# Two decoder layers on one core: buffer addresses, the order of transposes, copies and small loads at four places, and the last outputs by column halves

## The reference

```python
for i in range(2):
    h = rms_norm(x, attn_norm[i])
    proj = h @ w_in[i]                       # 1024 x 3072, six units of 512 columns
    sb = rms_norm(stick_breaking(sb_q, sb_k, sb_v), sb_out_norm[i])        # 8 heads of 64
    df = rms_norm(differential(df_q, df_k, df_v, bias, lam), diff_subln[i]) * (1 - lambda_init)
    x = x + concat(sb, df) @ w_out[i]
    h2 = rms_norm(x, ffn_norm[i])
    x = x + (swiglu(h2, dense...) if i == 0 else moe_top2_of_8(h2, router_w, experts...))
return rms_norm(x, final_norm)
```

## Time and profile before

| | |
|---|---|
| time, median of 3 runs | 1462.85 us (1462.66 to 1463.01) |
| the profiled execution's own time | 1462.97 us |
| its span (first to last instruction) | 1460.8 us, so 2.2 us lie around it |
| mean granted TensorE clock | 0.994 of full speed |
| TensorE, VectorE, ScalarE busy | 98%, 77%, 64% of the span |
| DMA | 448.81 MB, 307 GB/s over the span |

### The profile page before, as it was taken

The page is one execution under the profiler, slowest core; times in us unless marked ns, Lnnn a source line. Parts: engine busy times, 40 slices in busy tenths (PEclk is TensorE's granted clock), DMA queues, the critical chain, the costliest instruction groups (busy, mean ns, idle before and its releaser), DMA issues.

```text
span 1460.8 us, 18431 instructions
## 1 busy us (share of the span) xinstructions
PE 1434.2 (98%) x6979; PEld 1179.6 (81%) x6979; DVE 1127.8 (77%) x852; ACT 934.4 (64%) x753; POOL 32.5 (2%) x51
## 2 busy tenths in 40 slices
PE   7999999999999999999999999999999999999996
PEld 7977888889888788888888888888888888888885
DVE  5664545536856899888888888888888888888896
ACT  4454544435554777777777777777777777767774
POOL 0010000000010020000000000000000000001000
PEclk9999999999999999999999999999999999999999
DMA  9642895555433899999999999999999999999992
GB/s 332 211 144 87 321 361 182 173 191 178 150 116 101 289 369 399 394 378 384 357 376 376 363 381 360 384 356 382 373 355 384 375 361 372 369 385 360 396 386 81
DMA packets 190909, 448.81 MB, mean 307 GB/s; under 512 B 8516, under 2 KB 11403, under 8 KB 190859
## 3 DMA queue, kind: packets, MB, share of 16 engines
q1 hardware_dynamic: 189034, 442.27, 83.4%
q0 software_dynamic: 1616, 5.77, 1.0%
q10 hardware_dynamic: 208, 0.08, 0.0%
HBM read 429.74 MB, written 18.36 MB: 307 GB/s over the span
## 4 chain that ended last, share of the span: by engine, by line
PE 95%; DMA 2%; DVE 2%; ACT 1%; SPq 1%; issue 0%; DVEq 0%
PE ps L511 88%; PE ps L950 2%; DMA raw<-in_w_in 1%; PE ps L634 1%; DMA hn<-bias_scratch 1%; PE ps L658 0%; PE ps L908 0%; PE ps L681 0%; PE ps L592 0%; PE ps L786 0%; DMA bias_scratch<-vrow 0%; DVE w_lo L361 0%; PE ps L623 0%; PE ps L645 0%; PE ps L876 0%; PE ps L646 0%
## 5 line engine op out<-in xcount | busy, mean ns | idle before, releaser
L361 DVE TENSOR_TENSOR w_lo<-raw,w_hi 128x2048 fp32r<-128x2048 f32 x401 | 916.0, 2291 | 233.8 <-ACT w_hi L356 232.2
L356 ACT ACTIVATE w_hi<-raw 128x2048 fp32r<-128x2048 f32 (+1 forms) x401 | 767.6, 1915 | 332.3 <-PE ps L511 327.6
L511 PE MATMUL ps<-w_hi,xe_hi 128*128 128x512 f32 x896 | 249.6, 400 | 0.3 <-DVE xe_lo L1744 0.3
L511 PE MATMUL ps<-w_hi,xe_lo 128*128 128x512 f32 x896 | 245.4, 395 | 0.0
L511 PE MATMUL ps<-w_lo,xe_hi 128*128 128x512 f32 x896 | 244.8, 394 | 0.0
L511 PEld LDWEIGHTS ps<-w_lo,xe_hi 128*128 128x128 f32 x896 | 168.2, 188 | 41.1
L511 PEld LDWEIGHTS ps<-w_hi,xe_lo 128*128 128x128 f32 x896 | 168.2, 188 | 40.5
L511 PEld LDWEIGHTS ps<-w_hi,xe_hi 128*128 128x128 f32 x896 | 164.6, 188 | 36.9 <-issue 0.5
L511 PE MATMUL ps<-w_hi,he_hi 128*128 128x512 f32 x448 | 123.5, 397 | 0.0
L511 PE MATMUL ps<-w_hi,he_lo 128*128 128x512 f32 x448 | 122.7, 395 | 0.0
L511 PE MATMUL ps<-w_lo,he_hi 128*128 128x512 f32 x448 | 122.4, 395 | 0.0
(11 more groups left out here) (237 smaller groups left out, 991.5 us busy)
## 6 DMA issues: line engine op xcount, KB each, us to landing
raw<-in_expert_w_gate SPq DMA_DIRECT2D x112, 1024.0 KB, 7.4
raw<-in_expert_w_up SPq DMA_DIRECT2D x112, 1024.0 KB, 7.5
raw<-in_expert_w_down SPq DMA_DIRECT2D x112, 1024.0 KB, 7.2
raw<-in_w_in SPq DMA_DIRECT2D x24, 1024.0 KB, 7.2
raw<-in_dense_w_gate SPq DMA_DIRECT2D x11, 1024.0 KB, 6.4
...
```

Source lines behind the costliest of these rows:

```text
L356: nc.scalar.activation(w_hi[:, n % SPL, 0:width], raw[:, n % RAW, 0:width], ACT.Copy).then_inc(hi_ready, 1)
L361: nc.vector.tensor_tensor(w_lo[:, n % SPL, :], raw[:, n % RAW, :], w_hi[:, n % SPL, :].bitcast(F32), ALU.subtract).then_inc(lo_ready, 1)
L511: return pe.matmul(o, stationary, moving, start=start, stop=stop, skip_group_check=True)
```

## The change

- `gC`, 16 bytes per partition, becomes the beginning of `head_gains`, 64 bytes. SBUF buffers are laid one behind the other in steps of 32 bytes, so all that come after it move up by 32: `rw`, `cst` (the identity in it), `bias`, `aT_*`, `hT_*`, `xe_*`, `he_*`, `ye_*`, `onehotT`, `sil`, `hid`, `xrow` began 32 bytes past a multiple of 64 and now begin at one; some small ones (`row_ss`, `head_ss`, `diag`, `att`) do the opposite. `raw`, `w_hi`, `w_lo`, `xs`, `hn` stay, at multiples of 64.
- The start: TensorE turns x first, then the norm gains, then runs 8 products of no use instead of 8 and 16. Half of the norm rows come by GpSimd's queue instead of ScalarE's, and `gain` is loaded there last. ScalarE squares x ahead of piece 2; VectorE makes the root, `diag` and `vrow` ahead of piece 2's low part.
- The heads' rows are turned between the two tiles of `w_out(1)`.
- The router: x's other half is turned tile by tile between the `logits`, without the 6 products of no use; the experts' third piece is split later, on both engines; `rT`'s last copy goes ahead of a product with `gain`.
- The ending: the last expert piece pair is multiplied by column halves (`down_by_columns`), and conversion, scatter, addition and squares follow by halves; one root for both tiles; tile 0 is scaled by ScalarE and stored by SyncE, tile 1 is scaled by VectorE and stored by ScalarE's queue.

Twelve products moved from ahead of the transposes to behind them. The diff, cut to its core:

```diff
@@ -129,7 +129,8 @@
 gT = sb("gT", [P, 2 * DEPTH, KT])
-gC = sb("gC", [P, 2, DEPTH])
+head_gains = sb("head_gains", [P, P // 8])
+gC = head_gains[:, 0:2 * DEPTH].rearrange("p (a l) -> p a l", a=2)
 rw = sb("rw", [P, KT, NE])
@@ -434,20 +438,20 @@
                last_block=True)
-    for t in range(TT):
-        sp.wait_ge(out_rows, t + 1)
-        sp.dma_start(out[0, t * P:t * P + P, :], hn[:, t, :]).then_inc(out_sent, 16)
+    sp.wait_ge(out0_done, 1)
+    sp.dma_start(out[0, 0:P, :], hn[:, 0, :]).then_inc(out_sent, 16)
     sp.wait_ge(out_sent, 16 * TT)
...
 def _(pool):
-    pool.dma_start(gain[:], ffn_norm[DEPTH - 1].partition_broadcast(P)).then_inc(gain_in, 16)
+    pool.dma_start(norm_rows[DEPTH * KT:2 * DEPTH * KT, :], ffn_norm.rearrange("l (k p) -> (l k) p", p=P)).then_inc(ffn_rows_in, 16)
     pool.wait_ge(vrow_done, 1)
...
     pool.dma_start(bias_up, bass.AP(scratch.tensor, 0, [[1, P], [384, DF_HEADS], [1, S]])).then_inc(bias_in, 16)
+    pool.dma_start(gain[:], ffn_norm[DEPTH - 1].partition_broadcast(P)).then_inc(gain_in, 16)
@@ -595,11 +599,11 @@
 pe.wait_ge(ident_in, 16)
+turn_x(0, (0, 1, 2, 3), 4)
+pe.wait_ge(norms_in, 16)
+pe.wait_ge(ffn_rows_in, 16)
+pe.transpose(ps[:, 3, 0:2 * DEPTH * KT], norm_rows[:], ident[0:2 * DEPTH * KT, 0:2 * DEPTH * KT]).then_inc(gT_turned, 1)
 keep_running(8, 0)
-pe.wait_ge(norms_in, 32)
-pe.transpose(ps[:, 3, 0:2 * DEPTH * KT], norm_rows[:], ident[0:2 * DEPTH * KT, 0:2 * DEPTH * KT]).then_inc(gT_turned, 1)
-turn_x(0, (0, 1, 2, 3), 4)
-keep_running(16, 0)
 for l in range(DEPTH):
@@ -767,9 +771,10 @@
 w_out(0, (1,))
-w_out(1)
+w_out(1, (0,))
 pe.wait_ge(sb_rows, TT * (l + 1))
 turn_rows((0, 1))
+w_out(1, (1,))
 pe.wait_ge(t_lo, 12 * l + 8)
@@ -877,12 +882,14 @@
+pe.wait_ge(rT_done, 2)
+turn_x(2 * DEPTH - 1, (2, 3), tiles=(0,))
 pe.wait_ge(rw_ready, 1)
-pe.wait_ge(rT_done, 2)
-for k in range(4):
-    logits(k)
-keep_running(6, 1)
-turn_x(2 * DEPTH - 1, (2, 3))
+logits(0)
+logits(1)
+turn_x(2 * DEPTH - 1, (2, 3), tiles=(1,))
+logits(2)
+logits(3)
 pe.wait_ge(rT_done, 3)
@@ -969,6 +975,24 @@
+def down_by_columns(c):
+    pe.wait_ge(eh_lo, b * E_CH + c + 1)
+    for o in range(2):
+        for half in range(2):
+            n = MOE0 + AT[("down", c, half)]
+            hi = high(n, b)
+            for rows in (he_hi, he_lo):
+                for f in range(2):
+                    add(ps[:, 4 + o, :], rows[:, c % 2, 2 * half + f, :], hi[:, f * D + o * CH:f * D + o * CH + CH])
+            lo = low(n, b)
+            for f in range(2):
+                last = add(ps[:, 4 + o, :], he_hi[:, c % 2, 2 * half + f, :],
+                           lo[:, f * D + o * CH:f * D + o * CH + CH], stop=(half == 1 and f == 1))
+            if o == 1:
+                last.then_inc(piece_used, 1)
+        if o == 0:
+            last.then_inc(y_first, 1)
...
 for c in range(E_CH + 1):
@@ -1001,17 +1027,17 @@
 expert_block(final, False, last_block=True)
-pe.wait_ge(y_lo, 1)
 pe.wait_ge(hot_saved, 1)
-scatter(0)
-scatter(1, 0)
+for o in range(2):
+    pe.wait_ge(y_lo, o + 1)
+    for t in range(TT):
+        scatter(t, o)
...
 act.dma_start(norm_rows[0:DEPTH * KT, :], attn_norm.rearrange("l (k p) -> (l k) p", p=P)).then_inc(norms_in, 16)
-act.dma_start(norm_rows[DEPTH * KT:2 * DEPTH * KT, :], ffn_norm.rearrange("l (k p) -> (l k) p", p=P)).then_inc(norms_in, 16)
 steps = [0]
@@ -1082,8 +1108,8 @@
     split_hi(act, 1)
+    row_norms(0)
     split_hi(act, 2)
-    row_norms(0)
 else:
@@ -1224,10 +1250,10 @@
 square_rows(3, 0, junk[0])
-split_hi(act, MOE0 + 2)
 router_rows((2,))
...
 row_root(3)
+split_hi(act, MOE0 + 2)
@@ -1300,12 +1325,34 @@
 nc.scalar.preload_act_table_set("natural_log_exp_and_others")
-output_hi(blocks)
+act.wait_ge(y_first, 1)
+output_hi(0)
+act.wait_ge(piece_used, nth(MOE0, blocks))
+output_hi(1)
...
+def square_half(c, t, sums):
...
+    half = slice(c * CH, c * CH + CH)
+    act.wait_ge((x_c0, x_done)[c][t], 4)
+    nc.scalar.activation(y_of[:, 0, t, half], xs[:, t, half], ACT.Square,
+                         accum_out=sums[:, t:t + 1]).then_inc(row_ss_done, 1)
...
 for t in range(TT):
-    square_rows(4, t, hn[:, t, :])
+    square_half(0, t, row_s0)
+for t in range(TT):
+    square_half(1, t, row_ss)
+act.wait_ge(v0_done, 1)
+act.wait_ge(row_ss_done, TT * 6)
+for t in range(TT):
     one = slice(t, t + 1)
-    act.wait_ge(row_ss_done, TT * 4 + t + 1)
-    inverse_root(row_rstd[:, one], row_ln[:, one], row_ss[:, one], D).then_inc(row_rstd_done, 1)
+    last = nc.scalar.activation(row_ln[:, one], row_ss[:, one], ACT.Ln, scale=1.0 / D, bias=row_v0[:, one])
+link(last)
+nc.scalar.activation(row_rstd[:], row_ln[:], ACT.Exp, scale=-0.5).then_inc(row_rstd_done, 1)
+act.wait_ge(r_done, 5)
+act.wait_ge(xg_done, 2)
+copy(hn[:, 0, :], hn[:, 0, :], row_fine[:, 0:1]).then_inc(out0_done, 1)
+act.wait_ge(out_rows, 1)
+act.dma_start(out[0, P:2 * P, :], hn[:, 1, :]).then_inc(out_sent, 16)
@@ -1402,11 +1437,14 @@
     split_lo(dve, 1)
-    split_lo(dve, 2)
 root(2 * l)
...
 last.then_inc(diag_done, 1)
+if l == 0:
+    dve.wait_ge(vrow_mm, 1)
+    V.tensor_copy(vrow[:], ps[0:DF_HEADS, 3, 0:384]).then_inc(vrow_done, 1)
+    split_lo(dve, 2)
@@ -1459,9 +1497,6 @@
 split_lo(dve, n0 + 3)
-if l == 0:
-    dve.wait_ge(vrow_mm, 1)
-    V.tensor_copy(vrow[:], ps[0:DF_HEADS, 3, 0:384]).then_inc(vrow_done, 1)
 dve.wait_ge(rB_spread, l + 1)
@@ -1632,9 +1667,9 @@
 dve.wait_ge(x_done[1], 3)
-with_gain(1).then_inc(xg_done, 1)
 dve.wait_ge(t_done, 4 * 5 + 4)
 V.tensor_copy(both(rT[:, 6:8, :]), ps[:, 7, :]).then_inc(rT_last, 1)
+with_gain(1).then_inc(xg_done, 1)
@@ -1673,8 +1708,6 @@
-split_lo(dve, MOE0 + 2)
...
 def gates():
@@ -1744,16 +1777,18 @@
-def output_lo():
...
-    dve.wait_ge(y_hi, 1)
-    V.tensor_tensor(ye_lo[:], both(ps[:, 4:6, :]), ye_hi[:].bitcast(F32), ALU.subtract).then_inc(y_lo, 1)
...
-def add_back(b, t, bank=6):
...
-    dve.wait_ge(sc_done[t], 1)
-    return V.scalar_tensor_tensor(out=xs[:, t, :], in0=both(ps[:, bank:bank + 2, :]),
-                                  scalar=gate[:, t, bass.ds(b - 1, 1)], in1=xs[:, t, :], op0=ALU.mult, op1=ALU.add)
+def output_lo(o):
...
+    dve.wait_ge(y_hi, o + 1)
+    half = slice(o * CH, o * CH + CH)
+    V.tensor_tensor(ye_lo[:, half], ps[:, 4 + o, :], ye_hi[:, half].bitcast(F32), ALU.subtract).then_inc(y_lo, 1)
...
+def add_back(b, t, o):
...
+    dve.wait_ge(sc_done[t], o + 1)
+    half = slice(o * CH, o * CH + CH)
+    V.scalar_tensor_tensor(out=xs[:, t, half], in0=ps[:, (6, 0)[t] + o, :], scalar=gate[:, t, bass.ds(b - 1, 1)],
+                           in1=xs[:, t, half], op0=ALU.mult, op1=ALU.add).then_inc((x_c0, x_done)[o][t], 1)
@@ -1809,6 +1844,7 @@
 gathered(0)
+split_lo(dve, MOE0 + 2)
 expert_block(0, True)
@@ -1816,11 +1852,28 @@
 blocks = final + 1
-output_lo()
-add_back(blocks, 0).then_inc(x_done[0], 1)
-add_back(blocks, 1, 0).then_inc(x_done[1], 1)
-for t in range(TT):
-    normalise_last(t)
+output_lo(0)
+add_back(blocks, 0, 0)
+output_lo(1)
+add_back(blocks, 1, 0)
+add_back(blocks, 0, 1)
+add_back(blocks, 1, 1)
+dve.wait_ge(row_ss_done, TT * 5)
+mean_square(row_v0, row_s0, D).then_inc(v0_done, 1)
+dve.wait_ge(gain_in, 16 * 2)
+dve.wait_ge(x_c0[0], 4)
+dve.wait_ge(x_done[0], 4)
+V.tensor_tensor(hn[:, 0, :], xs[:, 0, :], gain[:], ALU.mult).then_inc(xg_done, 1)
+dve.wait_ge(v0_done, 1)
+dve.wait_ge(row_ss_done, TT * 6)
+link(V.scalar_tensor_tensor(out=row_var[:], in0=row_ss[:], scalar=1.0 / D, in1=row_v0, op0=ALU.mult, op1=ALU.add))
+dve.wait_ge(row_rstd_done, 5)
+refine(row_fine[:], row_rstd[:], row_var[:], row_tmp[:]).then_inc(r_done, 1)
+dve.wait_ge(r_done, 5)
+dve.wait_ge(x_c0[1], 4)
+dve.wait_ge(x_done[1], 4)
+V.scalar_tensor_tensor(out=hn[:, 1, :], in0=xs[:, 1, :], scalar=row_fine[:, 1:2],
+                       in1=gain[:], op0=ALU.mult, op1=ALU.mult).then_inc(out_rows, 1)
```

More of the change, by code:

```diff
@@ L245, in build @@
         x_blocks = x_rows.rearrange("(b p) d -> b p d", p=P)
+        row_s0, row_v0 = head_ss[:, 0:TT], head_var[:, 0:TT]
         y_blocks = y_rows.rearrange("(b p) d -> b p d", p=P)
@@ L259, in build @@
         rw_in = sem("rw_in")
-        gain_in, norms_in, gT_turned, gT_saved = (sem(n) for n in ("gain_in", "norms_in", "gT_turned", "gT_saved"))
+        gain_in, norms_in, ffn_rows_in = sem("gain_in"), sem("norms_in"), sem("ffn_rows_in")
+        gT_turned, gT_saved = sem("gT_turned"), sem("gT_saved")
         gC_turned, gC_saved = sem("gC_turned"), sem("gC_saved")
@@ L290, in build @@
             sem(n) for n in ("esilu_done", "ehid_done", "et_done", "eh_hi", "eh_lo"))
-        y_hi, y_lo = sem("y_hi"), sem("y_lo")
+        y_first, y_hi, y_lo = sem("y_first"), sem("y_hi"), sem("y_lo")
+        v0_done, out0_done = sem("v0_done"), sem("out0_done")
         sc_done = [sem("sc_done0"), sem("sc_done1")]
@@ L579, in turn_rows, with turn_x @@
                             last.then_inc(t_done, 1)
-            def turn_x(m, pairs, bank=6):
-                for t in range(TT):
+            def turn_x(m, pairs, bank=6, tiles=range(TT)):
```

(19 more changed lines are left out.)

10 lines of the change are left out of this document (removed).

## The result

The changed kernel takes 1421.79 us (median of 4 runs, 1420.26 to 1423.22), the one before on the same chip 1462.76 (1462.49 to 1463.01): a ratio of 0.972, 95% interval 0.9703 to 0.9737. It is faster by 41.0 us where 18.2 were forecast. The profiled execution took 1421.18, its span is 1418.1, its granted clock 0.997.

What follows compares the result with a forecast made beforehand. TensorE, holding the last chain for 95% of the span, was taken as the bound. Terms 8.3 + 6.1 + 2.4 + 1.4 = 18.2 us gave 1444.8 (1444.7 on the median's scale); own range 1440 to 1449, with rivals 1432 to 1451.

Steps and rivals of the forecast that it cites:

- The addresses, 0: All TensorE products: moving buffers to multiples of 64 bytes was taken as worth 0, with 26 us either way for rivals.
- The other estimate on record, 91 us: 5160 products of 512 columns: if addresses caused the 17.6 ns above the Trainium skill's 215.7, 91 us; held for unlikely.
- products get faster by their addresses: Rival for products with weights: operands at the same place in 64 bytes run faster, 26 us more, 1419; chance 0.17.
- The schedule terms: Gains from the changed order at start, heads' rows, router and ending: 18.2 us in sum.
- start: Start of the kernel: piece 0 begins earlier, the `vrow` wait and slow products behind it go, bias in time: 8.3 us.
- heads' rows, layer 0: Layer 0, transposes of heads' rows: TensorE's 2.17 us stop and its 1.64 us slow tail go; 3.8 us.
- heads' rows, layer 1: Layer 1, transposes of heads' rows: the 2.17 us stop and a tail of about 0.1 go; 2.3 us.
- router: From the router's logits to the experts: experts begin at 473.0 instead of 475.34, 2.4 us, bounds 1.5 to 2.6.
- ending: After the last expert products: rows ready 2.65 us sooner, less 1.3 for simultaneous outputs; 1.4 us, bounds 0.3 to 2.7.
- its term of 4.9: Part of the start: the 3.2 us wait for `vrow` and 1.7 us of slow products behind it go.
- a stop moves rather than goes: Rival at heads' rows and bias: TensorE still stands over 1 us at two; 5 to 6 us return, 1450; chance 0.10.

Runs made afterwards that it cites:

- m1: Separate kernel computing nothing of the model: TensorE products with operands shifted in steps, other engines still; 512 columns took 229.0 ns at difference 0, 235.0 at 128.
- e1: The kernel before with only the padding that moves the buffers behind gC to multiples of 64 bytes: 1439.76 us against 1462.56.
- e6: The changed kernel with all activations moved 64 bytes further: 1414.33 us, ratio 0.9684.
- e12: The changed kernel with only the dense layer's hidden units and the experts' activations moved 64 bytes further: 1412.10 us against 1461.76.
- e2: The changed kernel without the padding, so the new order with the old addresses: 1444.68 us, ratio 0.9873.
- e7: The changed kernel with TensorE's first instructions in the old order: 1422.97 us, ratio 0.9738.
- e8: The changed kernel with row norms and `vrow` behind the splits again, ScalarE's and VectorE's old order at the start: 1428.86 us, ratio 0.978.
- e9: The changed kernel with the heads' rows turned behind both tiles of `w_out(1)` again, in both layers: 1427.67 us against 1461.77.
- e10: The changed kernel with the router's old order on all three engines: 1423.08 us, ratio 0.9736.
- e11: The changed kernel with the old ending, by whole rows, a root per tile, both stores by SyncE: 1422.75 us, ratio 0.9735.
- e3: The kernel before with weights and activations both 32 bytes past a multiple of 64: 1439.11 us, ratio 0.9844.

## Why the prediction was wrong

**The failed step is "The addresses, 0".** I had the two prices in hand, 233.3 ns in the dense stretch and 228.3 ns for the scatter's products, and set the difference aside because the latter use one stationary matrix four times. By the table of m1 the scatter's operands lie 13312 and -9216 bytes apart, both multiples of 256, the dense ones at 160. Reuse need not be called on, though it was not tried by itself. The term was 22.8 us (e1 against before); 5160 x 4.2 ns make 21.7 of it. What is left is small but no single thing: the products of 256 columns, which the forecast did not price at all, got faster too (144 in 16.35 us instead of 17.09), and the 0.4 us that such products won ahead of the wait for `vrow` were lost in it. The error was not in the sum but in the choice: between two ends 26 us away on either side I took the middle, although one row spoke for the faster end and none for the slower one. The other estimate on record, 91 us, hung on 17.6 ns per product; of these even the best difference gives back only 6.4 (233.3 to 226.9).

The rival *products get faster by their addresses* had the right sign, and nearly the right time, 1419 against 1421.79, with a chance of 0.17. Its reason was half wrong. It said that both operands at the same place in 64 bytes give the pace of 228.3; by that rule a difference of 128 would be as good as 0, and m1 has 235.0 ns for it against 229.0. The change went from a difference of 160 to one of 192, to a better value and not to the best, as e6 and e12 show.

**The schedule terms were right in sum, and all but the router's within 0.4 us.** Without the padding the changed kernel takes 1444.68; the forecast was 1444.7. That the two agree to the last digit is luck: e2's four times go from 1443.40 to 1445.71, and the misses of two terms offset each other in part. The milestones of e2 against those of before give each term where it arises:

| term | forecast | e2, by milestones | undone alone (span; medians) |
|---|---|---|---|
| start | 8.3 | 46.45 - 38.19 = 8.3 | 2.8; 1.2 (e7, piece 0) and 9.0; 7.1 (e8, `vrow`) |
| heads' rows, layer 0 | 3.8 | (142.85 - 130.64) - 8.3 = 3.9 | both layers: |
| heads' rows, layer 1 | 2.3 | (457.04 - 442.56) - 12.2 = 2.3 | 5.0; 5.9 (e9) |
| router | 2.4 | (475.34 - 459.82) - 14.5 = 1.0 | 2.7; 1.3 (e10) |
| ending | 1.4 | 17.3 - 15.5 = 1.8 | 1.7; 1.0 (e11) |

e8 is larger than its term of 4.9 because the 3 us that the start gains turn into a wait there: 5.3 us instead of 3.2.

The router is the one term that e2 missed, by 1.4 us. The changed kernel itself has it: 475.34 - 457.04 = 18.30 us from the second transposes to the experts before, 450.88 - 435.24 = 15.64 now, 2.7 less. In e2 the same stretch took 17.26; its traced execution is the longest of its four. The windows of that stretch (from:to, us, busy times, then granted clock, DMA share, GB/s), e2 from the last logits on, and the changed kernel:

```profile
448.00:451.00 3.00, 3.00 (x26) 3.00 (x25) 1.82 (x2) 2.94 (x6) 0.55 (x1) 0.83 0.17 68
451.00:454.00 3.00, 3.00 (x19) 2.94 (x19) 2.43 (x13) 0.94 (x1) 0.00 (x0) 0.50 0.43 175
454.00:460.00 6.00, 6.00 (x45) 6.00 (x42) 2.65 (x12) 2.08 (x3) 0.00 (x0) 0.76 0.00 0
```

```profile
440.60:443.20 2.60, 2.60 (x27) 2.60 (x25) 1.82 (x2) 2.54 (x6) 0.22 (x1) 1.00 0.27 110
443.20:446.00 2.80, 2.80 (x18) 2.74 (x17) 2.35 (x13) 1.37 (x1) 0.34 (x1) 0.50 0.52 181
446.00:450.90 4.90, 4.90 (x47) 4.90 (x45) 2.72 (x13) 2.08 (x3) 0.00 (x0) 0.93 0.01 3
```

TensorE falls to its lower level (1.2 GHz) behind the logits in both, without having waited; in e2 it fell earlier and stayed longer. From the last 24 logits to the experts e2 takes 11.87 us (447.95 to 459.82), the changed kernel 10.29 (440.59 to 450.88), and that is where the router's miss lies. The forecast had no term for that. Whether e2's other executions lose it too, no trace shows.

**The rival "a stop moves rather than goes"** did not come about: no wait of TensorE above 1 us is new in e2 or in the changed kernel.

**What stays open.** Why the pace goes by the difference modulo 256, and why its values lie as they do (0 and 16 good, 32 to 160 bad, 192 better), no run here tells; the records of the weight loads beside the experts' products do not change (188 ns on average in these traces). Nor is it known why 144 products of 256 columns at one difference take 113.5 ns each in e1 and e3 and 117.8 in the changed kernel. The differences 144 and 176 were not tried, both operands were moved together by 32 and 64 bytes only, and all products measured are of float32r.
